# Gates' projection as a token-major Strassen product of 2x2 blocks, run first, with the gates kept in HBM

## The reference, cut to what matters

```python
h = _rmsnorm(x, norm_g[layer])
proj = h @ w_in[layer]                       # 2048 x 10304
aq, ak, av, ag, cq, ckv, kr, bg, mg = jnp.split(proj, SPLIT_POINTS, axis=-1)
...
oa = _diff_attention(...)                    # branch A, 8 heads
ya = (oa.reshape(b, s, A_WIDTH) * jax.nn.silu(ag)) @ w_oa[layer]
...
ob = _mla_attention(q_nope, q_rope, k_nope, k_rope, vb)   # branch B, 8 heads
yb = (ob.reshape(b, s, B_WIDTH) * jax.nn.silu(bg)) @ w_ob[layer]

ga, gb = jnp.split(mg, 2, axis=-1)           # the gates: mg is 512 x 4096
merged = jax.nn.sigmoid(ga) * ya + jax.nn.sigmoid(gb) * yb
x = x + merged @ w_out[layer]
return _rmsnorm(x, final_g)
```

## Time and profile before

| | |
|---|---|
| median of 3 runs | 1507.8 us (1507.7 to 1508.03) |
| profiled execution | 1507.93 us, span 1506.1 us, mean granted clock 0.999 |
| PE busy | 1485.6 us, 99% of the span |
| DVE busy | 765.5 us, 51% |
| ACT busy | 518.5 us, 34% |
| DMA | 140.46 MB, mean 93 GB/s |

### The profile page before, as it was taken

The page is one execution under the profiler, slowest core; times in us unless marked ns, Lnnn a source line. Parts: engine busy times, 40 slices in busy tenths (PEclk is TensorE's granted clock), DMA queues, the critical chain, the costliest instruction groups (busy, mean ns, idle before and its releaser), DMA issues.

```text
span 1506.1 us, 19432 instructions
## 1 busy us (share of the span) xinstructions
PE 1485.6 (99%) x6996; PEld 1242.0 (82%) x6996; DVE 765.5 (51%) x1157; ACT 518.5 (34%) x781; POOL 35.1 (2%) x58
## 2 busy tenths in 40 slices
PE   6999999999999999999999999999999999999997
PEld 5888888888888888888888888888888888888886
DVE  6667566666656547777778232222223222253431
ACT  6333434434433334434445222222222222242321
POOL 0000000000000000000000000000000000000000
PEclk9999999999999999999999999999999999999999
DMA  6322222222222332222222333333333333344422
GB/s 197 95 71 84 70 84 72 81 82 72 78 75 84 85 98 77 64 70 63 70 63 70 99 98 98 96 91 94 96 97 97 97 97 97 97 154 154 153 98 112
DMA packets 236277, 140.46 MB, mean 93 GB/s; under 512 B 18640, under 2 KB 223568, under 8 KB 235728
## 3 DMA queue, kind: packets, MB, share of 16 engines
q1 hardware_dynamic: 236240, 139.97, 32.0%
HBM read 135.74 MB, written 4.19 MB: 93 GB/s over the span
## 4 chain that ended last, share of the span: by engine, by line
PE 97%; issue 1%; DMA 1%; DVE 0%; ACT 0%; SPq 0%; POOLq 0%; POOL 0%; DVEq 0%; ACTq 0%
PE bank L1241 30%; PE bank L1243 30%; PE bank L1242 30%; PE bank L1296 2%; PE bank L1270 1%; PE bank L1273 1%; DMA w_raw<-in_w_in_dram 1%; PE bank L1327 1%; PE bank L1321 1%; PE bank L1292 0%; PE bank L1288 0%; PE bank L1289 0%; PE bank L1291 0%; PE bank L1287 0%; PE bank L1350 0%
## 5 line engine op out<-in xcount | busy, mean ns | idle before, releaser
L770 DVE TENSOR_TENSOR w_lo<-w_raw,w_hi 128x1024 fp32r<-128x1024 f32 (+1 forms) x238 | 288.3, 1211 | 534.8 <-ACT w_hi L451 533.9
L1241 PE MATMUL bank<-h_hi,w_hi 128*128 128x512 f32 x1296 | 509.6, 393 | 0.5 <-DVE k_hl L775 0.3
L1243 PE MATMUL bank<-h_hi,w_lo 128*128 128x512 f32 x1296 | 504.9, 390 | 0.0
L1242 PE MATMUL bank<-h_lo,w_hi 128*128 128x512 f32 x1296 | 504.7, 389 | 0.0
L451 ACT ACTIVATE w_hi<-w_raw 128x1024 fp32r<-128x1024 f32 (+1 forms) x238 | 249.9, 1050 | 569.3 <-DMA w_raw<-in_w_in_dram 340.1
L1243 PEld LDWEIGHTS bank<-h_hi,w_lo 128*128 128x128 f32 x1296 | 243.3, 188 | 51.5
L1241 PEld LDWEIGHTS bank<-h_hi,w_hi 128*128 128x128 f32 x1296 | 243.5, 188 | 49.9 <-DVE k_hl L775 0.7
L1242 PEld LDWEIGHTS bank<-h_lo,w_hi 128*128 128x128 f32 x1296 | 243.6, 188 | 48.3
L471 ACT ACTIVATE e<-e,small 128x512 f32<-128x512 f32 x64 | 45.8, 716 | 139.5 <-DVE small L801 139.5
L1241 PE MATMUL bank<-w_hi,mg_hi 128*128 128x512 f32 x224 | 87.1, 389 | 0.0
L1242 PE MATMUL bank<-w_lo,mg_hi 128*128 128x512 f32 x224 | 87.1, 389 | 0.0
(11 more groups left out here) (175 smaller groups left out, 1627.2 us busy)
## 6 DMA issues: line engine op xcount, KB each, us to landing
w_raw<-in_w_in_dram SPq DMA_DIRECT2D x324, 256.0 KB, 3.1
w_raw<-in_w_out_dram SPq DMA_DIRECT2D x56, 256.0 KB, 2.8
w_raw<-in_w_oa_dram SPq DMA_DIRECT2D x32, 256.0 KB, 2.9
w_raw<-in_w_ob_dram SPq DMA_DIRECT2D x32, 256.0 KB, 2.9
x_tok<-in_x_dram SPq DMA_DIRECT2D x7, 1024.0 KB, 6.9
w_raw<-in_w_ukv_dram SPq DMA_DIRECT2D x16, 256.0 KB, 3.0
e_raw<-in_w_out_dram SPq DMA_DIRECT2D x8, 256.0 KB, 3.5
out_dram<-x_tok SPq DMA_DIRECT2D x8, 256.0 KB, 2.6
```

Of the source, the lines that this page charges most:

```text
L770: dve.tensor_tensor(w_lo[:, piece.slot, 0:cols], w_raw[:, piece.slot, 0:cols], w_hi[:, piece.slot, 0:cols].bitcast(F32), ALU.subtract).the ...
L1241: pe.matmul(dst, lhs_hi, rhs_hi, start=start, stop=False)
L1242: pe.matmul(dst, lhs_hi, rhs_lo, start=False, stop=False)
L1243: return pe.matmul(dst, lhs_lo, rhs_hi, start=False, stop=stop)
```

## The change

It has three parts.

**1. Gates' projection first, as a 2x2 Strassen product (7 block products instead of 8).** `h` is cut into 2 halves of 256 tokens x 2 halves of 1024 channels (A11, A12, A21, A22), and the 4096 gate columns into `M_GROUPS` = 4 groups of 1024, in each of which the weights are 2 halves of channels x 2 halves of 512 columns. It is the form with combinations S1 to S4 of `h` (made once: DVE S1, GpSimd S2, S3 and S4) and T1 to T4 of the weights (made by DVE for every weight tile), seven products P1 to P7, and sums of them. The work goes in 72 steps (`MergeStep`), each with its own raw buffer of 128x2048 (4 of them, `m_raw`), one of 3 high parts (`m_hi`), and the low part over the raw one (`m_lo`). A step's kind says what it multiplies at one channel tile k:

- P (steps 0 to 7): one product, two tiles k, 12 matmuls, no weight sums, 1024 wide
- A0 (8 to 15): 3 products, 18 matmuls, 3 sums, 1536 wide
- B0 (16 to 23): 2 products, 12 matmuls, 1 sum, 1024 wide
- X (8 in each of the groups 1 to 3): 3 products, 18 matmuls, 2 sums, 1536 wide
- Y (8 in each of these groups): 4 products, 24 matmuls, 3 sums, 2048 wide

Every matmul is 128x512, with tokens on the partitions. For a step n DVE makes the sums over the raw tile (`merge_sums`, 128x512 each), then ACT the high part (`merge_hi`), then DVE the low part (`merge_lo`), then PE multiplies. At a group's end DVE adds the products out of PSUM in seven sums of 128x1024 (`sum_u2`, `sum_w`, `sum_u3_c22`, `sum_c12`, `sum_c21`, `sum_c11`), ACT copies P1 and P2 out (`keep_p1`, `keep_p2`), takes the sigmoids and writes the gates to HBM (`gate_out`, 4 DMAs of 512 KB a group). Steps 0 to 7 run while tokens 256 to 511 are still being normalised and turned.

**2. Branch outputs token-major.** After branch B, `y_block` makes `ya` and `yb` in 8 units of 512 columns x 512 tokens (32 pieces of `w_oa` and `w_ob`, 24 matmuls each, as many as before). SP loads the gates back, 1 MB a unit (`gates_in`); DVE multiplies and adds (`gate_y`, `add_y`).

**3. `merged` turned by PE.** The output projection needs `merged` with channels on the partitions, so PE turns it in 64 transposes of 128x128 (`turn_merged`), and ACT and DVE split it out of PSUM.

The heads of branch A and B, the latent projections and the output projection keep their code; buffers move to other places in SBUF. Positions, distances and lambda are now set up during the first head of branch A. The diff, cut to its core:

```diff
--- before.py
+++ after.py
+class MergeStep:
+    def __init__(self, n):
+        self.n = n
+        self.raw, self.hi = n % M_RAW, n % M_HI
+        self.landed = 32 * (n // M_RAW + 1)
+        if n < 8:
+            self.kind, self.g, self.k = "P", 0, 2 * (n % 4)
+        elif n < 24:
+            self.kind, self.g, self.k = ("A0", "B0")[n >= 16], 0, n % 8
+        else:
+            self.kind, self.g, self.k = ("X", "Y")[(n - 24) % 16 >= 8], 1 + (n - 24) // 16, n % 8
+        self.first = self.k == 0
+        self.final = self.k == (6 if self.kind == "P" else 7)
+        p0, p1 = {"P": (0, 2), "A0": (1, 4), "B0": (0, 2), "X": (0, 3), "Y": (0, 4)}[self.kind]
+        self.cols = slice(p0 * SEQ, p1 * SEQ)
...
+N_MERGE = 24 + 16 * (M_GROUPS - 1)
+MERGE = [MergeStep(n) for n in range(N_MERGE)]
...
+UNIT_PAIR = [0, 1, 2, 3, 4, 5, 6, 7, 0, 4, 1, 5, 2, 6, 3, 7]
+UNIT_BANK = [2, 3, 4, 5, 6, 7, 2, 3, 4, 5, 6, 7, 2, 3, 6, 7]
+EARLY_UNITS = 6
+TURN_X_AT = {0: (6,), 1: (7,), 3: (8, 9), 4: (10, 11), 5: (12, 13), 6: (14, 15)}
...
+            def merge_piece(n):
+                st = MERGE[n]
+                if n >= M_RAW:
+                    sp.wait_ge(m_used, n - (M_RAW - 1))
+                raw = m_raw[:, st.raw, :]
+                col = MG + st.g * GROUP
+                def block(r, c0, width):
+                    return w_in[0, r * P:(r + 1) * P, col + c0:col + c0 + width]
+                top, low = st.k, st.k + HALF_K
+                if st.kind == "P":
+                    r = low if n >= 4 else top
+                    parts = [(raw[:, j * SEQ:(j + 1) * SEQ], block(r + j, 0, SEQ)) for j in range(2)]
+                elif st.kind in ("A0", "Y"):
+                    parts = [(raw[:, 0:2 * SEQ], block(top, 0, GROUP)), (raw[:, 2 * SEQ:4 * SEQ], block(low, 0, GROUP))]
+                elif st.kind == "B0":
+                    parts = [(raw[:, 0:SEQ], block(top, SEQ, SEQ)), (raw[:, SEQ:2 * SEQ], block(low, SEQ, SEQ))]
+                else:
+                    parts = [(raw[:, 0:2 * SEQ], block(top, 0, GROUP)), (raw[:, 2 * SEQ:3 * SEQ], block(low, SEQ, SEQ))]
+                for dst, src in parts:
+                    sp.dma_start(dst, src).then_inc(m_in[st.raw], 16)
...
+            def full_a(m):
+                pool.wait_ge(h_lo_ready, m + 1)
+                k = 2 * m
+                dst = s34_raw[:, k % HALF_K:k % HALF_K + 2, k // HALF_K, :]
+                pool.tensor_tensor(dst, h_hi[:, k:k + 2, 0:HALF_T].bitcast(F32), h_lo[:, k:k + 2, 0:HALF_T].bitcast(F32),
+                                   ALU.add).then_inc(f_ready, 1)
+            def combine(j):
+                ks = slice(2 * j, 2 * j + 2)
+                s1, s2 = s12_raw[:, ks, 0, :], s12_raw[:, ks, 1, :]
+                s3, s4 = s34_raw[:, ks, 0, :], s34_raw[:, ks, 1, :]
+                pool.wait_ge(s1_ready, j + 1)
+                if j == 0:
+                    pool.wait_ge(f_ready, KT // 2)
+                pool.tensor_tensor(s2, s1, s3, ALU.subtract).then_inc(s2_ready, 1)
+                pool.wait_ge(s2_ready, j + 1)
+                pool.tensor_tensor(s4, s4, s2, ALU.subtract).then_inc(s4_ready, 1)
+                pool.tensor_tensor(s3, s3, h_raw[:, ks, HALF_T:SEQ], ALU.subtract).then_inc(s3_ready, 1)
...
+            def merge_hi(n):
+                st = MERGE[n]
+                if st.kind == "P":
+                    act.wait_ge(m_in[st.raw], st.landed)
+                else:
+                    act.wait_ge(m_sum, n - 7)
+                if n >= M_HI:
+                    act.wait_ge(m_used, n - (M_HI - 1))
...
+            def merge_step(n):
+                if n < N_MERGE and MERGE[n].kind == "X" and MERGE[n].final:
+                    keep_p1(MERGE[n].g)
+                if n + AHEAD < N_MERGE:
+                    merge_hi(n + AHEAD)
+                if n < N_MERGE and MERGE[n].kind == "Y" and MERGE[n].final:
+                    keep_p2(MERGE[n].g)
+                if n == 9:
+                    gate11(0)
+                if 8 <= n < 11:
+                    late_hi(n - 7)
+                if 10 <= n < 14:
+                    s34_hi_of(n - 10)
+                if 33 <= n < 37:
+                    late_hi(n - 29)
+                for g in range(M_GROUPS):
+                    end = 23 + 16 * g
+                    if n == end + 1:
+                        gate22(g)
+                    if n == end + 2:
+                        gate12(g)
+                    if n == end + 3:
+                        gate21(g)
+                    if g and n == end + 4:
+                        gate11(g)
...
-            def sigmoid(i, b, branch):
-                first = M0 + 6 * b + 2 * branch + 2
-                act.wait_ge(used, i * M_STEPS + first)
-                act.activation(sig[:, b, branch, :], bank[(0, 4)[b] + branch][:, :], ACT.Sigmoid
-                               ).then_inc(sig_ready, 1)
-            def merge_step(s, i):
-                if s in (2, 4, 8, 10):
-                    b = s // 6
-                    if s % 6 == 2 and not isinstance(i, int):
-                        act.wait_ge(merged_ready, i * 2 + (b - 1))
-                    sigmoid(i, b, (s % 6) // 4)
+            quarter_hi(0)
...
+            def merge_lo(n):
+                st = MERGE[n]
+                dve.wait_ge(m_hi_ready, n + 1)
+                dve.tensor_tensor(m_lo[:, st.raw, st.cols], m_raw[:, st.raw, st.cols],
+                                  m_hi[:, st.hi, st.cols].bitcast(F32), ALU.subtract).then_inc(m_lo_ready, 1)
+            firsts, seconds = [0], [0]
+            def merge_sums(n):
+                st = MERGE[n]
+                p = [m_raw[:, st.raw, i * SEQ:(i + 1) * SEQ] for i in range(4)]
+                def first(dst, a, b, n_first=1):
+                    firsts[0] += 1
+                    dve.tensor_tensor(dst, a, b, ALU.subtract).then_inc(m_first, 1)
+                dve.wait_ge(m_in[st.raw], st.landed)
+                if st.kind == "X":
+                    first(p[1], p[1], p[0])
+                    dve.wait_ge(m_first, firsts[0])
+                    dve.tensor_tensor(p[2], p[2], p[1], ALU.subtract).then_inc(m_sum, 1)
+                elif st.kind == "Y":
+                    first(p[1], p[3], p[1])
+                    first(p[0], p[0], p[2])
+                    dve.wait_ge(m_first, firsts[0])
+                    dve.tensor_tensor(p[0], p[0], p[1], ALU.add).then_inc(m_sum, 1)
+                elif st.kind == "A0":
+                    first(p[1], p[1], p[0])
+                    dve.wait_ge(m_first, firsts[0])
+                    seconds[0] += 1
+                    dve.tensor_tensor(p[3], p[3], p[1], ALU.subtract).then_inc(m_second, 1)
+                    dve.wait_ge(m_second, seconds[0])
+                    dve.tensor_tensor(p[2], p[3], p[2], ALU.subtract).then_inc(m_sum, 1)
+                else:
+                    dve.tensor_tensor(p[0], p[1], p[0], ALU.subtract).then_inc(m_sum, 1)
+            def unit_lo(i):
+                dve.wait_ge(h_hi_ready, i + 1)
...
+            def merge_step(n):
+                if n + 1 < N_MERGE:
+                    merge_lo(n + 1)
+                if n + AHEAD < N_MERGE:
+                    merge_sums(n + AHEAD)
+                if n == 8:
+                    sum_c11(0)
+                if 8 <= n < 11:
+                    late_lo(n - 7)
+                if 11 <= n < 15:
+                    s34_lo_of(n - 11)
+                if 33 <= n < 37:
+                    late_lo(n - 29)
+                for g in range(M_GROUPS):
+                    end = 23 + 16 * g
+                    if n == end - 8:
+                        sum_u2(g)
+                        sum_w(g)
+                    if n == end:
+                        sum_u3_c22(g)
+                        sum_c12(g)
+                    if n == end + 1:
...
-            def branch_b(i, b):
-                n = i * 2 + (b + 1)
-                dve.wait_ge(used, i * M_STEPS + (M0 + 6 * b + 6))
-                dve.wait_ge(sig_ready, i * 4 + (2 * b + 2))
-                dve.tensor_tensor(part[:, 1, :], bank[4 * b + 3][:, :], sig[:, b, 1, :], ALU.mult).then_inc(part_b, 1)
-                dve.wait_ge(part_a, n)
-                dve.wait_ge(part_b, n)
-                dve.tensor_tensor(merged[:, bass.ds(i * (2 * SEQ) + b * SEQ, SEQ)], part[:, 0, :], part[:, 1, :],
...
+            def product(st, dst, which, part_no, start, stop, k=None):
+                c = slice(part_no * SEQ, (part_no + 1) * SEQ)
+                for j in range(2):
+                    hi, lo = block_of(which, st.k if k is None else k, j)
+                    last = three(dst[:, j * SEQ:(j + 1) * SEQ], hi, lo, m_hi[:, st.hi, c], m_lo[:, st.raw, c],
+                                 start, stop)
...
+            for n in range(N_MERGE):
+                st = MERGE[n]
+                last = merge_product(n)
+                last.then_inc(m_used, 1)
+                for i in TURN_X_AT.get(n, ()):
+                    turn_whole(i)
...
```

(31 more changed lines are left out.)

883 lines of the change are left out of this document (669 added, 214 removed).

## The result

The changed kernel takes **1564.76 us** in the median (1563.85 to 1565.67), the kernel before 1507.8: ratio **1.0376**, 95% interval 1.0355 to 1.0396. A fourth execution took 2478.67 us at a mean granted clock of 0.557; it counts in the median but not in the ratio, and the other three alone have 1563.86. The kernel is slower, as forecast, and the chain forecast for each step is there, but by 57 us where 20 were predicted: most of the 38 us between the two come from places that the prediction priced at nothing or next to it.

A forecast was written before the change was run, and what follows sets the result against it. PE bounds the kernel. 192 fewer matmuls save 43.3 us, but the start and serial chain put A's first head 11.7 us later; with +7.0 for transposes and about +1, +19.7 on 1507.9 gives 1528 us, range 1500 to 1548.

The forecast's parts named there:

- PE's pace as the bound before: Kernel before: PE busy for 99% of the span, 443 matmuls in 100 us, so 0.2257 us of PE each.
- The serial chain of sums, high and low part: Every gate step: DVE, ACT, DVE in turn, X 4.64, Y 6.19, A0 5.37, B0 2.95 us, longer than PE's work; 72%.
- the signs of being wrong: Profile after: `m_lo` 4.1 and 5.4 us apart, PE waiting for x or GpSimd's combinations, or heads starting far from 383.
- The rival that PE keeps pace: Gate steps: the chain is no longer than PE's steps, so the kernel is faster, 1474 us; 14%.
- Then S1 and S2 are there when ACT comes to them, and it costs nothing.: Start: GpSimd's 20 additions, taken as 1.1 us each, lie beside the other work and cost nothing.
- The rival of the prediction that names this: Start: GpSimd and DVE hinder each other, 1.24 us per `combine` instruction, step 8 comes 15 us later, 1543 us; 10%.
- the late low parts fit: Gate steps: late low parts behind the sums in DVE's queue fall into ACT's time and fit there.
- The sentence that ACT's sigmoids stand where it is free: Gate steps: ACT's sigmoids, copies and DMA issues stand behind a high part, where ACT is free for 3 us.
- Entering the branch outputs ... about +1.: Entry of the branch outputs: DVE splits four quarters of branch A's outputs between branch B's last softmaxes, about +1 us.
- Transposes of `merged` +7, heads and the rest unchanged.: After the gates: 64 transposes add 7.0 us on PE's path; heads, projections and tail keep 443 matmuls in 100 us.
- Loads are hidden.: Y steps: a landing of up to 13 us is hidden; the late-loads rival said 1550 us, 2%.
- PE's clock.: Gate steps: granted clock stays 1.00; the rival that it falls to its lower level said 1716 us, 2%.

The follow-up runs named there:

- the run that parts the early columns: Changed kernel with each step's high and low part made in two instructions, first the columns that need no sum, then the rest: 1526.61 us.
- the run with everything at once: Changed kernel with early columns parted, late high parts first, branch outputs' split and ACT's last quarter reordered, additions on DVE, no warm-up products: 1502.05 us.
- small additions: Changed kernel with GpSimd's additions on 4 of 256 columns, S2, S3 and S4 left out but for these: 1552.45 us.

## Why the prediction was right and wrong

- **PE's pace as the bound before; 0.2257 us a matmul; 192 fewer.** The pace was right: with the waits mended PE makes 440 in 100 us. Of the 43.3 us only 13.5 reach the first head even then, the rest goes into PE's further waits, most of them at the start, and in part into its clock there.
- **The serial chain of sums, high and low part.** Right, to 0.02 us a step: 4.64, 6.21, 5.37 and 2.95 against 4.64, 6.19, 5.37 and 2.95, each worked out from durations and handovers in a kernel that had no such chain. The first step behind a group's end takes 6.58 us, +1.9 for 2.0 forecast. Groups 2 and 3 take 89.2 us each, for 89.0. PE was idle for 46.5 us between 47 and 383, for 54 forecast; of the signs of being wrong the spacing of `m_lo` did not come, but the heads start at 413 instead of 383. The rival that PE keeps pace is refuted, and the run that parts the early columns shows that it is the order, not the amount of work, that costs: 38 us.
- **"Then S1 and S2 are there when ACT comes to them, and it costs nothing."** This is the step that failed most: GpSimd was priced by its own duration and taken as hidden. It took 1.3 to 2.7 us an addition (1.9 in the mean), not 1.1, and it lengthened DVE's own instructions by 0.5 to 1.1 us. Without it step 8 is done 12.3 us earlier, of the start's 16.3. The rival of the prediction that names this had 10% and happened: it put 1.24 us on each of twelve combinations, 15 in all; DVE's instructions beside them are 1.0 to 1.1 us longer, and the twelve cost 9 us. Another 2.9 are the warm-up products, which I had not put ahead of the turns of x's second tile. One more us stays unexplained. The Trainium skill (SBUF — State Buffer, Who interferes with whom) says that a DVE instruction with two SBUF inputs contends with a GpSimd one that reads SBUF, and one with a single SBUF input does not; the trace agrees on both, as the last section shows. The trace also fits what the prediction wrote of the interface, that it is held for a whole instruction.
- **"... and the late low parts fit."** Wrong. Their durations fit; their place does not. A late part stands behind the high part on ACT and ahead of the low part on DVE, so it lengthens the very chain that the prediction described: by 1.1 us in six steps and by 4.1 in the one with the sigmoid, 10.7 in all. Moving ACT's copy gave 10.9 us. I applied the serial rule to the sums and not to the other pair with the same shape. The sentence that ACT's sigmoids stand where it is free failed with it.
- **"Entering the branch outputs ... about +1."** Mis-sized: 8.3 us. The order of the queues was read for `quarter_lo` but not for the split ahead of the last softmax, whose load waits for PE itself. 5.7 us are PE's wait; the other 2.6 fit the 5 us at a granted clock of 0.50 right behind it.
- **Transposes of `merged` +7, heads and the rest unchanged.** Right: from the first head to the first branch matmul 768.7 us in the changed kernel, and 374.0 us from there on in the run with everything at once; 1142.7 in all, for 1143.1.
- **Loads are hidden.** Nearly true of the changed kernel (one wait of 0.6 us on DVE, in step 28), but with nothing to spare for an order that wants them a step earlier.
- **PE's clock.** It was 1.00 in the steady steps, as expected, but 0.77 to 0.83 at 40 to 100 us and 0.83 at 140 to 160, behind PE's wait of 5.3 us for the sums at a group's end. What that cost is not shown: PE waited there for DVE in any case.

Of the 38 us that were missing, the runs account for 12.3 (GpSimd up to step 8), 2.9 (warm-up), 10.9 (late parts) and 8.3 (split), 34.4. Two more are GpSimd's in step 9 (7.5 us in the changed kernel, 5.5 with small additions), and 0.7 is the wait for a load in step 28 (5.34 us instead of 4.64). The last one stays open.

## What to carry to other kernels

When a sum is put ahead of a high and low split, write down the relay engine by engine: if the first and the third leg stand on the same queue with nothing between them, the step costs the sum of all three, however idle both engines look. Part what does not need the sum before reordering across steps, since a deeper look-ahead may only swap the wait for the engine against one for the load. And once such a rule is found, apply it to every pair of the same shape, and price a helper engine by what it does to its neighbour's instructions, not by its own duration alone.
